# First layer, tile 0: half of the value rows gathered among the late key rows, inside tile 1's recurrence

## The chip, the core and the metric

The kernel is one program on one core of a Trainium2 chip. Its five engines work side by side and are ordered by semaphores alone: PE (TensorE, matmuls), DVE (VectorE), ACT (ScalarE), POOL (GpSimd, which issues the gathers here) and SP (SyncE, which issues the plain loads). The metric is device time in microseconds, from the first to the last instruction of the program with what lies around it; the median of several executions counts.

## What is computed

Two layers over 256 prompt tokens and 32 sample tokens: layer 0 mixes by an RWKV-7 recurrence, layer 1 by chunked gated linear attention, and after each stands a PEER mixer, in which every token has 8 heads x 16 = 128 experts. What the change touches is layer 0's recurrence for tile 1 and layer 0's PEER for tile 0:

```python
def step(S, inp):                       # RWKV-7, by token
    rt, wt, kt, vt, at, bt = inp
    sa = jnp.einsum('bhvk,bhk->bhv', S, at)
    S = S * wt[:, :, None, :] + sa[..., None] * bt[:, :, None, :] + vt[..., None] * kt[:, :, None, :]
    yt = jnp.einsum('bhvk,bhk->bhv', S, rt)
...
ue = jnp.take(u, expert, axis=0)        # PEER: key rows of the chosen experts
act = jax.nn.gelu(jnp.einsum('thed,td->the', ue, xt), approximate=False)
ve = jnp.take(v, expert, axis=0)        # and their value rows
return jnp.einsum('the,thed->td', (gate * act).astype(xt.dtype), ve)
```

## The kernel before, in words

The 288 tokens are three tiles: 0 and 1 of 128 prompt tokens, 2 (SAMPLE) with the 32 sample tokens in four copies. For a prompt tile each of the 128 experts of a token is one column: one gather by POOL brings 128 rows of 1024 float32 (0.52 MB), one for each token, into a slot of SBUF. Four gathers are a round. A tile has 32 key rounds (side 0, from `peer_u`) and 32 value rounds (side 1, from `peer_v`).

**The ring.** Until late in the program there are two groups of four slots. `round_at` gives every round its place n in the order of all rounds, `place_of(n)` its group; successive rounds alternate between the two. POOL walks the order in `gather` (line 721 issues) and, before it refills a slot, waits until that slot was used. Its queue is in order, so a gather that waits holds all behind it. For tile 0 of layer 0 all 32 key rounds stand before all 32 value rounds.

**Who uses the rows.** A key row is used by DVE in `row_product` (line 1125: one multiply and sum over 1024 columns). A value round is used by PE in `value_round`: eight matmuls of 32 lanes x 512 columns (line 1920) into `total`, which is PSUM banks 6 and 7. It waits for its four rows, and frees their slots as it goes through them.

**How they are spread.** Rows and rounds are no loops of their own: they are slipped into other work by a credit. On DVE `open_rows` opens a count and a rate, and `serve` spends rate x work whenever DVE is about to wait for a PSUM product (`fill`) or for ScalarE (`scalar_done`). On PE `open_values` does the same, and `serve` spends it ahead of each product for DVE (`for_vector`), each product for ScalarE (`for_scalar`) and each wait for operands (`operands`). With `paired`, only `fill` and `for_vector` spend credit, so that both engines count the same products. `rest_rows` and `rest_values` do what is left. Everything is decided when the program is built: on each engine the order is fixed.

**The place.** Tile 0's first 64 key columns are used during tile 1's input mixing. Then `core(1)` runs, tile 1's recurrence: for either half of the heads an attention part (five products for DVE), with the state and value matmuls behind each, then six levels of a triangular inverse (four products each, the last two) and the four closing products. In it DVE uses key columns 64 to 127 (`RATES["core1"]`, 1.9 rows for one unit of work). At its end PE opens the 32 value rounds at 0.5. `out(0, (1,))` follows: output product, norm, queries, scores and, in two halves, the choice of tile 1's experts; between scores and fan-out PE runs up to 6 more value rounds in each half, with 5 clock-raising matmuls behind each. A fan-out (`fan_out`) turns the chosen indices around for the value gathers; DVE waits for both (`experts_fanned`). Then comes `core(SAMPLE)`, which does the rest of the rounds before the sample's attention part, and in which DVE adds the sum of tile 0's experts (`add_experts`).

**PSUM banks.** ScalarE's products take two pairs of banks, (4, 5) and (6, 7), while `banks.two` holds, else the first alone. Since `total` is the second pair, `two` must be off when value rounds run. PE and ACT each keep their own count of it. Before, it goes off at the end of `core(1)`; with one pair, a product of 1024 columns waits until ScalarE has copied out the one before.

Of the kernel before, what the change touches and what calls it, by code (L numbers as in the profile page):

```python
# [54 lines left out]

MINGLED = ()

# [120 lines left out]
def program(nc, a, outs):  # L178
    (y_p, y_s, S_p, sh_p, G_p, S_s, sh_s, G_s) = outs
    with ExitStack() as ctx:  # L180
# [562 lines left out]
        def _(act):  # L743
# [119 lines left out]
            def core(t):  # L863

                sample = t == SAMPLE
                copy_out(wlog, D, func=ACT.Sigmoid)
                copy_out(bT, D, func=ACT.Sigmoid)
# [62 lines left out]
                if t == 1:  # L930
                    weights_due(0, 0, 1)
                    banks.two = False
                    copy_out(state_out[0][0:RK, :], D, RK)
                    act.dma_start(S_p[0, 0].rearrange("h v k -> v h k"),
                                  state_out[0][0:RK, :].rearrange("v (h k) -> v h k", k=RK)).then_inc(state_stored[0], 16)
                    nst[0] += 16
                    act.wait_ge(state_stored[0], nst[0])
# [150 lines left out]
        def _(dve):  # L1088
            w = Counts()
            stream = Share()  # L1090
            RATES = {"mix": 14, "core1": 1.9, "core2": 4.0, "enter": 6, "gla": 2.6, "out": 7}
            at = [0, 0, 0]
# [253 lines left out]
            def core(t):  # L1346
# [52 lines left out]
                if t == 1:  # L1399
                    weights_due(0, 0, 0)  # L1400
                    open_rows(0, 0, 64, 64, RATES["core1"])
                if sample:
# [411 lines left out]
        def _(pe):  # L1814
            w = Counts()
            banks, bufs, stream = Banks(), Buffers(), Share()
            at = [0, 0, 0]
            VALUE_RATES = {"out": 0.5, "gla": 0.5, "core2": 0.8}
            nfv, nfa = [0], [0]
# [203 lines left out]
            def core(t):  # L2023
# [3 lines left out]
                if t == 0:  # L2027
                    pe.wait_ge(pack_loaded, 16 * 5)
                    lora2, g2 = lora2_first, g2_first
                else:  # L2030
                    pack = weight(5)
                    bufs.kept = pack
                    lora2, g2 = pack_views(pack)
                for i in range(2):
# [62 lines left out]
                for group in groups_of(t):  # L2097
# [9 lines left out]
                    if t == 1:  # L2107
                        for hh, b in halves:
                            mark = turn_half(hh)
                            if hh == 0:  # L2110
                                fan_weights(0, 0, 0)
                            pe.wait_ge(scalar_drained, mark)
                            attention(b)
# [135 lines left out]
                if sample:  # L2249
                    open_values(0, 1, VALUE_RATES["out"])  # L2250
                if t == 1:
                    fan_weights(0, 0, 1)
                    banks.two = False
                    open_values(0, 0, VALUE_RATES["out"])
                    operands()
# [263 lines left out]
```

## Time and profile before

| | us |
|---|---|
| median of 3 executions (2941.88 to 2962.33) | 2942.13 |
| the profiled execution | 2945.39 |
| its span, first to last instruction | 2943.5 |
| PE busy | 1921.0 (65%) |
| DVE busy | 1594.7 (54%) |
| POOL busy | 1323.4 (45%) |
| ACT busy | 280.3 (10%) |
| chain that ended last: PE, DVE, DMA, POOL | 30%, 24%, 21%, 12% |

The granted TensorE clock was 0.809 of full speed in the mean. The profile names engines, lines and tiles; a wait is shown with the engine or transfer that ended it. Since no engine and no share of the chain dominates, the average says little: a change in one stage has to be read in that stage. In the rows, a value round is a row of PE with `128*32 128x512 x16` (each matmul of float32 counts twice there), a clock-raising matmul reads `pick,ident`.

### The profile page before, as it was taken

The page shows a single profiled execution, that of the slowest core. Times are in us where ns is not written, and L with a number is a line of the kernel's source. Part 1 is how long each engine was busy: PE and PEld are TensorE (multiplying, and loading weights), DVE is VectorE, ACT ScalarE, POOL GpSimd, SP SyncE. Part 2 cuts the span into 40 slices and gives each one's busy share as a digit, 9 for nine tenths or more (in the row PEclk, how much of TensorE's full clock was granted, in tenths as well). Part 3 has the DMA queues.
Part 4 walks back from the last instruction along what each step waited for, and adds up shares of the span by engine and source line. Part 5 has one row for each costly group of instructions (what it writes and reads, how often), then busy time and mean ns, then how long its engine had stood idle before and what let it go on. Part 6 is the DMA issues. An engine that isn't in the chain of part 4 may idle for free.

```text
span 2943.5 us, 26768 instructions
## 1 busy us (share of the span) xinstructions
PE 1921.0 (65%) x10173; PEld 1231.3 (42%) x10173; DVE 1594.7 (54%) x2987; ACT 280.3 (10%) x442; POOL 1323.4 (45%) x1160
## 2 busy tenths in 40 slices
PE   5879857837968776657577758678257764453533
PEld 2469523327945435445245227363135433350100
DVE  4253376566752826967412146865961738766033
ACT  1111000020110010010100110001100000000000
POOL 0000012543543555655334235556754675467774
PEclk8989979968789987767798888889568986776876
DMA  8430586964679897767999878789878998899998
GB/s 275 172 130 2 189 308 202 362 238 137 202 266 348 302 325 254 242 217 235 331 355 347 315 253 322 273 281 399 294 275 340 406 386 310 279 353 371 409 409 325
DMA packets 303482, 841.78 MB, mean 286 GB/s; under 512 B 46062, under 2 KB 57246, under 8 KB 303356
## 3 DMA queue, kind: packets, MB, share of 16 engines
q0 software_dynamic: 165888, 604.05, 56.1%
q1 hardware_dynamic: 126900, 231.65, 22.3%
q10 hardware_dynamic: 10568, 4.38, 0.6%
q8 instruction: 82, 1.34, 0.2%
q14 instruction: 44, 0.36, 0.0%
HBM read 829.68 MB, written 10.31 MB: 285 GB/s over the span
## 4 chain that ended last, share of the span: by engine, by line
PE 30%; DVE 24%; DMA 21%; POOL 12%; issue 7%; ACT 3%; PEld 1%; SPq 0%; ACTq 0%; DVEq 0%; PEldq 0%; POOLq 0%
PE psum L1920 28%; POOL arena L721 9%; DVE arena L1125 9%; DVE arena L1105 6%; DMA arena<-in_peer_v,idx_v 6%; POOL wring L721 3%; DMA wring<-in_ada_w 3%; DMA wring<-in_gla_w_in 3%; DMA wring<-in_rw_w_rkv 2%; DMA hc<-in_peer_v,idx_v 2%; DMA wring<-in_peer_wq 1%; PE psum L1938 1%; DVE hT L1105 1%; DMA out<-arena 1%; DMA wring<-in_peer_v,idx_u 1%
## 5 line engine op out<-in xcount | busy, mean ns | idle before, releaser
L721 POOL DMA_INDIRECT arena<-in_peer_u,idx_u x560 | 740.9, 1323 | 1062.1 <-DVE acts L1125 492.7
L1920 PE MATMUL psum<-arena 128*32 128x512 f32 (+6 forms) x3662 | 610.2, 557 | 447.8 <-DMA arena<-in_peer_v,idx_v 170.5
L1125 DVE CUSTOM_DVE_ANT_0 arena<-arena,hc 128x1024 f32<-128x1024 f32 x544 | 644.1, 1224 | 90.6 <-DMA arena<-in_peer_u,idx_u 64.5
L721 POOL DMA_INDIRECT arena<-in_peer_v,idx_v x428 | 422.1, 986 | 461.4 <-PE psum L1920 340.7
L1920 PEld LDWEIGHTS psum<-arena 128*32 128x32 f32 (+2 forms) x3662 | 323.5, 170 | 665.4 <-issue 477.8
L1920 PE MATMUL psum<-pick,ident 128*128 128x256 f32 x1090 | 272.7, 405 | 47.2 <-DVEq L1376 39.2
L1920 PEld LDWEIGHTS psum<-pick,ident 128*128 128x128 f32 x1090 | 215.3, 203 | 132.6 <-issue 54.0
L1920 PE MATMUL psum<-wring,arena 128*32 128x512 f32 (+3 forms) x728 | 213.9, 663 | 77.8 <-DMA wring<-in_peer_v,idx_v 43.0
L1920 PE MATMUL psum<-hT,wring 128*128 128x128 f32 (+3 forms) x1824 | 237.9, 293 | 17.0 <-ACT arena L767 6.3
L1920 PEld LDWEIGHTS psum<-hT,wring 128*128 128x128 f32 (+1 forms) x1824 | 225.7, 198 | 40.0 <-issue 21.9
L1920 PE MATMUL psum<-wring,hT 128*128 128x512 f32 (+1 forms) x480 | 192.2, 560 | 13.5 <-DMA wring<-in_gla_w_in 10.2
L767 ACT ACTIVATE arena<-psum 128x512 f32<-128x512 f32 (+6 forms) x125 | 97.3, 779 | 876.4 <-PE psum L1920 646.4
L1920 PEld LDWEIGHTS psum<-wring,arena 128*128 128x128 f32 (+2 forms) x728 | 85.6, 172 | 202.4 <-issue 182.6
L1920 PEld LDWEIGHTS psum<-wring,hT 128*128 128x128 f32 x480 | 90.0, 207 | 114.8 <-issue 100.0
L1105 DVE TENSOR_TENSOR arena<-arena 128x1024 f32<-128x1024 f32 (+4 forms) x148 | 124.8, 843 | 16.0 <-ACTq L1007 5.5
L1920 PE MATMUL psum<-wring,cT 128*32 128x512 f32 x384 | 65.0, 816 | 71.4 <-DMA wring<-in_ada_w 51.3
L1125 DVE CUSTOM_DVE_ANT_0 arena<-arena,psum 128x1024 f32<-128x1024 f32 x16 | 19.5, 1221 | 138.4 <-DMA arena<-in_peer_u,idx_u 137.7
L1245 DVE MAX8 arena<-psum 128x8 f32<-128x128 f32 x64 | 19.1, 299 | 137.3 <-PE psum L1920 135.0
L1105 DVE TENSOR_TENSOR arena<-psum,vring 128x1024 f32<-128x1024 f32 x12 | 14.7, 1223 | 136.1 <-PE psum L1920 93.1
L1938 PE MATMUL psum<-ident,arena 128*128 128x128 f32 x148 | 28.6, 359 | 80.6 <-DVEq L1633 42.6
L721 POOL DMA_INDIRECT wring<-in_peer_v,idx_v x64 | 61.3, 958 | 19.5 <-issue 19.5
L1105 DVE TENSOR_TENSOR arena<-arena,psum 128x512 f32<-128x512 f32 (+2 forms) x45 | 35.1, 780 | 58.4 <-PE psum L1920 57.1
(231 smaller groups left out, 1789.1 us busy)
## 6 DMA issues: line engine op xcount, KB each, us to landing
wring<-in_ada_w SPq DMA_DIRECT2D x24, 2048.0 KB
wring<-in_peer_wq SPq DMA_DIRECT2D x24, 2048.0 KB
wring<-in_rw_w_rkv SPq DMA_DIRECT2D x12, 2048.0 KB
wring<-in_gla_w_in SPq DMA_DIRECT2D x12, 2048.0 KB
wring<-in_rw_wo SPq DMA_DIRECT2D x6, 2048.0 KB
wring<-in_gla_wo SPq DMA_DIRECT2D x6, 2048.0 KB
vring<-mod_d SPq DMA_DIRECT2D x22, 512.0 KB
arena<-in_peer_u,idx_u POOLq DMA_INDIRECT x560, 6.2
```

The source lines that it names most:

```text
L721: pool.indirect_dma_start(slot(s, n), None, v_rows if side else u_rows, bass.IndirectOffsetOnAxis(index, 0)).then_inc(rows_landed[s], 16)
L767: done(act.activation(dst, shaped(fill(cols)[0:rows, :], dst), func, scale=scale), scalar_drained)
L1105: done(dve.tensor_tensor(out, i0, i1, op), s)
L1125: dve.tensor_tensor_reduce(slot(s, n), slot(s, n), hidden(li, t), 1.0, 0.0, MUL, ADD, acts[:, (3 * li + t) % 2, col:col + 1]).then_inc(row ...
L1245: done(dve.max(vals[:, 0:8], src))
L1920: return nc.tensor.matmul(out, lhsT, rhs, start=start, stop=stop)
L1938: last = nc.tensor.transpose(ps[:, k * P:(k + 1) * P], src[:, k * P:(k + 1) * P], ident[:])
```

## The change

It sets `MINGLED = ((0, 0),)`. In the order of rounds, tile 0's key rounds 16 to 31 and value rounds 0 to 15 then alternate. `core(1)` opens those 16 value rounds on PE right behind the first fan-out of key weights, paired, at 0.45 rounds for one product for DVE; DVE's key rows become paired as well, at 1.8. Rounds left over are done at the end of `core(1)`, and the other 16 value rounds are opened where all 32 were. ScalarE's products use one pair of banks from the start of `core(1)` on, on both engines.

```diff
-MINGLED = ()
+MINGLED = ((0, 0),)
...
             def core(t):
                 sample = t == SAMPLE
+                if t:
+                    banks.two = False
                 copy_out(wlog, D, func=ACT.Sigmoid)
...
                     weights_due(0, 0, 1)
-                    banks.two = False
...
-            RATES = {"mix": 14, "core1": 1.9, "core2": 4.0, "enter": 6, "gla": 2.6, "out": 7}
+            RATES = {"mix": 14, "core1": 1.8, "core2": 4.0, "enter": 6, "gla": 2.6, "out": 7}
...
-                    open_rows(0, 0, 64, 64, RATES["core1"])
+                    open_rows(0, 0, 64, 64, RATES["core1"], True)
...
-            VALUE_RATES = {"out": 0.5, "gla": 0.5, "core2": 0.8}
+            VALUE_RATES = {"core1": 0.45, "out": 0.5, "gla": 0.5, "core2": 0.8}
...
                     bufs.kept = pack
+                    banks.two = False
...
                                 fan_weights(0, 0, 0)
+                                open_values(0, 0, VALUE_RATES["core1"], 16, 0, True)
...
                 if t == 1:
+                    rest_values()
                     fan_weights(0, 0, 1)
-                    banks.two = False
-                    open_values(0, 0, VALUE_RATES["out"])
+                    open_values(0, 0, VALUE_RATES["out"], 16, 16)
```

POOL's gathers, in which the buffers of the ring are all named arena. Before, from the first one on:

```order
L721 DMA arena<-in_peer_u,idx_u 128x1024 x128
L721 DMA arena<-in_peer_v,idx_v 128x1024 x128
```

Now (where lines are left out, four gathers of either kind go on alternating):

```order
L721 DMA arena<-in_peer_u,idx_u 128x1024 x68
L721 DMA arena<-in_peer_v,idx_v 128x1024 x4
L721 DMA arena<-in_peer_u,idx_u 128x1024 x4
...
L721 DMA arena<-in_peer_v,idx_v 128x1024 x68
```

So 64 value gathers stand between key gathers, and a key gather now waits behind value gathers too.

PE in the third level of the recurrence: two level products for ScalarE (128x128), then four products for DVE (128x64). Before:

```order
L1920 MATMUL psum<-arena 128x128 x8
L1920 MATMUL psum<-wring,hT 128x128 x8
L1920 MATMUL psum<-arena,hT 128x64 x8
L1920 MATMUL psum<-hT,arena 128x64 x8
L1920 MATMUL psum<-arena,wring 128x64 x8
L1920 MATMUL psum<-wring,arena 128x64 x8
```

Now, with two value rounds (32x512) ahead of two of the products:

```order
L1921 MATMUL psum<-arena 128x128 x8
L1921 MATMUL psum<-wring,hT 128x128 x8
L1921 MATMUL psum<-arena,hT 128x64 x8
L1921 MATMUL psum<-arena 32x512 x8
L1921 MATMUL psum<-hT,arena 128x64 x8
L1921 MATMUL psum<-arena,wring 128x64 x8
L1921 MATMUL psum<-arena 32x512 x8
L1921 MATMUL psum<-wring,arena 128x64 x8
```

There are 16 such rounds between the first attention part's second product and the last product of the recurrence: two in each attention part, twelve behind.

PE from the last scores of `out(0, (1,))` to the sample's mixing (a value round is 32x512, `arena,pick` is a fan-out, `wring,arena` the sample's first product). Before, from the last round of the first half's choice on:

```order
L1920 MATMUL psum<-arena 32x512 x8
L1920 MATMUL psum<-pick,ident 128x256 x5
L1920 MATMUL psum<-arena,pick 128x64 x4
L1920 MATMUL psum<-arena 32x512 x8
L1920 MATMUL psum<-pick,ident 128x256 x5
...
L1920 MATMUL psum<-arena 32x512 x8
L1920 MATMUL psum<-arena,pick 128x64 x4
L1920 MATMUL psum<-wring,arena 128x512 x2
L1920 MATMUL psum<-arena 32x512 x8
L1920 MATMUL psum<-wring,arena 128x512 x2
```

Now, from the third and last round of that half on:

```order
L1921 MATMUL psum<-arena 32x512 x8
L1921 MATMUL psum<-pick,ident 128x256 x5
L1921 MATMUL psum<-arena,pick 128x64 x8
L1921 MATMUL psum<-wring,arena 128x512 x4
L1921 MATMUL psum<-arena,le 128x512 x2
```

The second half's fan-out follows the first's, and the sample's mixing starts, with no value round between.

## Rows read from the trace of the kernel before

**Rows 1.** Stages: us, busy of each engine, granted clock, DMA share, GB/s.

```profile
core 0: us, PE busy (x) PEld busy (x) DVE busy (x) ACT busy (x) POOL busy (x), PEclk, DMA share, GB/s
661.50:746.00 84.50, 66.44 (x365) 63.25 (x366) 48.28 (x61) 6.88 (x13) 25.41 (x20) 0.76 0.38 125
746.00:842.00 96.00, 86.62 (x662) 85.66 (x661) 81.07 (x126) 13.74 (x15) 58.51 (x44) 0.87 0.72 241
...
1022.00:1060.00 38.00, 25.21 (x133) 11.67 (x132) 0.85 (x4) 1.68 (x6) 19.69 (x21) 0.87 0.84 300
```

**Rows 2.** Chain of work that ended last: start, us, what.

```profile
1033.79 6.13 DMA arena<-in_peer_v,idx_v
...
1047.45 6.47 DMA arena<-in_peer_v,idx_v
```

**Rows 3.** Order of time, PE, the expert choice: start, us, matmuls, idle before, releaser.

```profile
1000.33 1.92 PE L1920 MATMUL psum<-arena 128*32 128x512 f32 x16 [2.08 <-DMA arena<-in_peer_v,idx_v]
...
1012.33 1.93 PE L1920 MATMUL psum<-arena 128*32 128x512 f32 x16 [1.02 <-DMA arena<-in_peer_v,idx_v]
...
1026.40 3.42 PE L1920 MATMUL psum<-arena 128*32 128x512 f32 x16 [3.73 <-DMA arena<-in_peer_v,idx_v]
...
1054.06 3.24 PE L1920 MATMUL psum<-arena 128*32 128x512 f32 x16 [4.02 <-DMA arena<-in_peer_v,idx_v]
1057.23 1.10 PE L1920 MATMUL psum<-arena,pick 128*128 128x64 f32 x8
```

**Rows 4.** Order of time, POOL, value gathers in the same stage.

```profile
1014.48 1.88 POOL L721 DMA_INDIRECT arena<-in_peer_v,idx_v  x1 [1.47 <-PE psum L1920]
...
1030.07 0.94 POOL L721 DMA_INDIRECT arena<-in_peer_v,idx_v  x1 [4.51 <-PE psum L1920]
1031.31 0.94 POOL L721 DMA_INDIRECT arena<-in_peer_v,idx_v  x1 [0.30 <-issue]
```

**Rows 5.** Order of time, DVE, from the second half's indices to the sample's mixing.

```profile
1021.33 0.19 DVE L1700 CAST idx_u<-arena 128x64 uint32<-128x64 f32 x1
...
1059.71 0.23 DVE L1751 CAST idx_v<-arena 128x128 uint32<-128x128 f32 x1 [36.60 <-ACTq L983]
1073.35 1.23 DVE L1105 TENSOR_TENSOR arena<-arena,vring 128x1024 f32<-128x1024 f32 x1 [13.41 <-DMA vring<-in_rw_kk]
...
1081.86 0.17 DVE L1108 TENSOR_SCALAR s<-s 128x16 f32<-128x16 f32 x1 [4.67 <-ACTq L772]
...
1103.35 1.23 DVE L1105 TENSOR_TENSOR arena<-psum,vring 128x1024 f32<-128x1024 f32 x1 [3.31 <-PEq L1852]
```

**Rows 6.** DMA issues, 746 to 842, then 975 to 1060: count, median us to landing.

```profile
arena<-in_peer_u,idx_u POOLq DMA_INDIRECT x36, 5.8
...
arena<-in_peer_v,idx_v POOLq DMA_INDIRECT x51, 6.2
```

**Rows 7.** Order of time, PE, first level's products and the closing ones.

```profile
748.38 1.90 PE L1920 MATMUL psum<-arena,hT 128*128 128x64 f32 x16
750.12 1.95 PE L1920 MATMUL psum<-hT,arena 128*128 128x64 f32 x16
...
832.17 9.10 PE L1920 MATMUL psum<-arena 128*128 128x64 f32 x80
```

**Rows 8.** Order of time, ACT, the copy of a level's first product.

```profile
761.98 1.02 ACT L767 ACTIVATE arena<-psum 128x1024 f32<-128x1024 f32 x1 [12.31 <-PE psum L1920]
```

**Rows 9.** Order of time, attention parts: POOL's gathers, DVE's and PE's last products.

```profile
673.95 1.68 POOL L721 DMA_INDIRECT arena<-in_peer_u,idx_u  x1 [0.64 <-DVE acts L1125]
...
676.02 2.05 PE L1920 MATMUL psum<-arena 128*128 128x128 f32 x16 [1.50 <-DVE hc L1105]
...
681.85 1.22 DVE L1105 TENSOR_TENSOR hc<-psum,le 128x1024 f32<-128x1024 f32 x1
...
713.10 1.68 POOL L721 DMA_INDIRECT arena<-in_peer_u,idx_u  x1 [20.39 <-DVE acts L1125]
...
723.40 1.22 DVE L1105 TENSOR_TENSOR hc<-psum,le 128x1024 f32<-128x1024 f32 x1
```

## The prediction

> **What bounds the kernel now.** I read the stage table first, then the chain of work that ended last, then the order of time on PE, POOL and DVE. Around the change no one engine is the bound everywhere [rows 1]. In the levels of tile 1's recurrence (746 to 842) PE is busy 86.62 of 96 us and DVE 81.07; the DMA engines have a share of 0.72, and only key rows fly. In the two attention parts (661.5 to 746) the DMA share is 0.38. Later it turns over: from 1022 to 1060 DVE is busy 0.85 of 38 us. There the chain alternates between value gathers in flight and PE's rounds: a last gather of four flies 6.13 us, the next one's 6.47 [rows 2], and a round follows when its four rows have landed, 12.0 us after the round before it in the same four slots (1000.33 to 1012.33) or 14.07 (1012.33 to 1026.40) [rows 3]. PE fans out the second half's expert indices only at 1057.23, behind six such rounds [rows 3], though DVE had written that half by 1021.33 + 0.19 = 1021.52; DVE then waits 36.60 us [rows 5]. So the value rows are short of time there, and the recurrence has DMA time over. The change trades one against the other.
>
> **What it gives.** Of 32 value rounds 16 move into the recurrence. Behind it stand the same 13 rounds up to the last score product, then 3 instead of 6 in the first half's choice, 0 instead of 6 in the second's, and 0 instead of 7 around the fan-out and in the start of the sample's mixing. Terms:
> - The second fan-out follows DVE's write at 1021.52 and not the round of 1054.06: about 1022 instead of 1057.23, 35 us.
> - DVE's start into the sample's mixing then waits 13.41 us for rw_kk [rows 5], behind a semaphore that comes with the fan-out; it moves along. Its next wait, 4.67 us for ScalarE's root, hangs on PE products among which two rounds stood: between 0 and 4.67, I take 4, since both rounds leave.
> - The 3.31 us in which DVE waited for the last value sum [rows 5] go: the last of the 32 rounds then stands third in the first half's choice, long before.
> Together 42 us. Bounds: 35 + 0 + 3.3 = 39 and, with the whole 4.67 and a rw_kk load that is somewhat quicker without gathers beside it, 46. The DMA work is not less: the moved gathers just fly earlier.
>
> **What it costs.** The 36 PSUM products between PE and DVE in the recurrence (10 of attention, 20 of levels one to five, 2 of level six, 4 at the end) pace both sides: 1.8 key rows and 0.45 value rounds each. Key and value rounds alternate in the gather order, so from here on key rows live in one group of four slots and value rows in the other. There is no second group for values: a round's four gathers can start only when PE has used the round before, and POOL, in order, issues them only behind the four key gathers ahead of them.
>
> The price of that loop, from rows: POOL starts 0.27 us after a round's end (1030.07 after 1026.40 + 3.42); gathers start 1.24 us apart at best (0.94 + 0.30), three steps are 3.72 [rows 4]; the last lands 5.8 us after its issue in the levels, 6.2 later on (medians) [rows 6]; the round is 1.92 us at full clock, 3.42 otherwise [rows 3]. Sum 11.7 at best. Measured loops of this kind are 12.0 and 14.07 [rows 3], the long one when a gather took 1.88 us instead of 0.94 [rows 4]. In the levels POOL is such a POOL: 58.51 us for 44 gathers is 1.33 each [rows 1], and eight of 1.33 + 0.30 are 13.0 us per key and value round. I take 13.0, between the two measured loops and with POOL's own price.
>
> Levels: value round 4 stands ahead of the second product of level one, now at 750.12; round 15 stands ahead of the last product, which now starts at 832.17 + 24/40 of 9.10 = 837.6 [rows 7] (24 of its row's 40 matmuls come before it). Between lie 11 loops: 750.12 + 11 x 13.0 + 1.92 = 895.0, against 837.6: **+57 us**. DVE's rows (1.8 instead of 1.9 per product) and PE's own work fit inside: 2.2 products between rounds are some 8 of the 13 us on DVE (81.07 us over 26 products is 3.1 each, and a level's rows get fewer).
>
> Attention: round 0 is there early, round 1 is wanted before the fifth product. POOL may start on it only after the key gather of 673.95, which waited for the fourth key row: 675.93, three steps of 1.24 to 1.98, 5.8 in flight, a round of 1.92 to 3.42, a product of 2.05: 689 to 693, where DVE took that product at 681.85: +7.5 to +11. In the second half the same from the gather of 713.10, with two products behind: 731 to 734 against DVE's 723.40: +7 to +11 [rows 9]. Twice 9: **+18 us**. PE's stretches between (state and values) do not shorten.
>
> The single PSUM pair: the second level product of a pair now waits for ScalarE's copy of the first (starts at 761.98, 1.02 long [rows 8]); with the hand-overs I put it at 1.4 us, six times, 8 in all, and twice for the turns. I cost it at nothing, since PE waits for value rows in each loop anyway; without that cover it would be 8.
>
> Sum: 18 + 57 - 42 = **+33 us**. The profiled execution took 2945.39 us (span 2943.5), 3.3 above the median of 2942.13. I add the difference to the median: 2975 us.
>
> **A rule against the trace.** Thirteen loops (11 in the levels, one in each attention part) each hold a gather's flight of 5.8 us [rows 6]. The Trainium skill, DMA: Bandwidth & Descriptors, section "Anatomy of one DMA — SWDGE (gpsimd) path", fits a DMA from GpSimd as 2.0 us plus its bytes at 436 GB/s; for 0.52 MB that is an estimate of 3.2 us, 2.6 less than the row. By it the loop would be 10.4 and the change would come out even. The row decides, since it counts from POOL's issue to the landing, as the loop does.
>
> **Rivals.** With a loop of T us the cost is 18 - 2 x (13 - T) + 750.12 + 11 T + 1.92 - 837.6 = 13 T - 93.6, and the change costs nothing at T = 10.4.
> - *Loop at its floor* (T = 12.0): cost 62, net +20, 2962. For it: rounds at full clock and gathers of 0.94 do run so [rows 3, 4]. Against: in the levels a gather takes 1.33 on average [rows 1].
> - *Even*: shorter flights or partial overlap bring T to 10.4 or so: net 0, 2942. For it: DMA share only 0.72 [rows 1]. Against: flights are 5.8 us under that light load [rows 6]. (The fit of the Trainium skill above would give this case.)
> - *Faster*: the moved rounds fall into DMA time that is idle, and the recurrence hardly stretches. It decides at T = 8.2, where the cost is 13 and the net -29: 2913 us; at the 7.8 us that the 11 loops have today (837.6 - 750.12 = 87.5, less a round, over 11) it would be the whole gain less the attention parts. For it: 0.38 and 0.72 of DMA share. Against: a loop holds a flight, three steps and a round, 11.7 at best.
> - *POOL slowed throughout* (T = 14.07): cost 89, net +47, 2989. For it: the row of 1.88 and the 1.68 of the attention part [rows 4, 9]. This is the upper end of the forecast's case.
>
> **How the numbers follow.** A change of 1% is 29 us, about what a measurement of this kernel tells from none; slower by over 1% begins at T = 12.7. Of the measured loops' spread (12.0 to 14.07) two thirds lie above. Chances: loop of 12.7 to 14.1, my forecast, 0.52; floor case 0.26; even case 0.14; faster 0.08. So faster 0.08, within 1% 0.40, slower 0.52. The range reaches from the even case (2944) to the slow loop with the smaller gain (2942 + 89 - 39 = 2992); what is left out is the faster case, a little of the even one and something above. The forecast's own part of it is 2971 to 2992.
>
> **What the changed profile would show.** Right: the stretch from the first attention product to the second half's key weights (661.5 to 843) about 75 us longer; in it PE waiting for in_peer_v rows ahead of nearly each value round, same-slot rounds 12 to 14 us apart, DVE waiting for PE's PSUM; DMA share near 0.8 there; the 36.60 us wait on the second fan-out gone to about 1 or 2; no value round behind the first half's choice; from the recurrence's end to the first attention product of the sample's mixing about 42 us less. Wrong: rounds less than 12 us apart, so the loop is not what binds; PE waiting for vector_drained or for ScalarE's copies rather than for rows; or a gain that ends before DVE's start into the sample's mixing because a load (rw_kk, recurrent rows) arrives no earlier.

## The result, and the profile after

| | before | after |
|---|---|---|
| median, us | 2943.47 (4 executions, 2941.88 to 2962.33) | 3023.15 (4 executions, 3014.87 to 3028.63) |
| span of the profiled execution, us | 2943.5 | 3018.7 |
| granted TensorE clock, mean | 0.809 | 0.794 |

The ratio is 1.0238, with a 95% interval of 1.0204 to 1.0271: the change costs 2.4%, some 70 us. The two medians lie 79.7 us apart, which is the upper end of that interval; the two profiled spans differ by 75.2. The kernel before is itself not steady to better than 29 us: over all its executions, those of the experiments included, it took 2940 to 2970 us, so each ratio compares a kernel with runs of before on the same chip.

Stages after (columns as in [rows 1]): the attention parts, the levels with the closing products, the stretch up to the second fan-out, the start of the sample's mixing.

```profile
core 0: us, PE busy (x) PEld busy (x) DVE busy (x) ACT busy (x) POOL busy (x), PEclk, DMA share, GB/s
662.80:768.40 105.60, 72.24 (x418) 59.58 (x417) 47.79 (x59) 6.88 (x13) 36.82 (x35) 0.73 0.50 174
768.40:944.40 176.00, 116.18 (x864) 87.66 (x864) 84.90 (x130) 13.73 (x15) 102.45 (x93) 0.83 0.79 273
944.40:1124.60 180.20, 109.47 (x690) 64.85 (x690) 88.36 (x247) 12.93 (x22) 62.80 (x64) 0.82 0.75 272
1124.60:1182.00 57.40, 24.82 (x71) 15.96 (x72) 29.03 (x35) 14.17 (x20) 5.54 (x4) 0.50 0.28 90
```

Where the forecast had all of the recurrence's added time in waits for rows, PE waits for two things there: the rows of value rounds, and ScalarE's copies. What PE waited for from the first attention product to the second half's key weights, in sum, times and longest, before:

```profile
PE psum L1920 <- DVEq L1434: 8.8, 2, 5.0
PE psum L1920 <- DVE hT L1105: 8.4, 5, 2.3
...
PE psum L1920 <- ACT hT L767: 2.1, 1, 2.1
```

And after:

```profile
PE psum L1921 <- DMA arena<-in_peer_v,idx_v: 70.8, 11, 11.7
PE psum L1921 <- ACT arena L767: 9.5, 8, 1.3
...
PE psum L1939 <- ACT arena L853: 2.6, 1, 2.6
```

70.8 us for value rows are new, and so are ScalarE's copies: 9.5 + 2.6 and two smaller ones (1.2 and 0.8) are 14.1 us, where before only one of 2.1 us stood.

Order of time on PE after, levels three to six (columns as in [rows 3]; value rounds are the rows of 128x512):

```profile
836.94 1.92 PE L1921 MATMUL psum<-arena 128*32 128x512 f32 x16 [0.18 <-DMA arena<-in_peer_v,idx_v]
...
853.72 3.26 PE L1921 MATMUL psum<-arena 128*32 128x512 f32 x16 [6.02 <-DMA arena<-in_peer_v,idx_v]
...
867.31 3.29 PE L1921 MATMUL psum<-arena 128*32 128x512 f32 x16 [6.62 <-DMA arena<-in_peer_v,idx_v]
...
880.65 1.92 PE L1921 MATMUL psum<-arena 128*32 128x512 f32 x16 [1.21 <-ACT arena L767]
...
893.15 3.64 PE L1921 MATMUL psum<-arena 128*32 128x512 f32 x16 [6.86 <-DMA arena<-in_peer_v,idx_v]
896.72 2.32 PE L1921 MATMUL psum<-arena,wring 128*128 128x64 f32 x16
898.88 1.95 PE L1921 MATMUL psum<-wring,arena 128*128 128x64 f32 x16
900.66 2.00 PE L1921 MATMUL psum<-arena 128*128 128x128 f32 x16
903.93 2.02 PE L1921 MATMUL psum<-wring,hT 128*128 128x128 f32 x16 [1.26 <-ACT arena L767]
905.79 1.90 PE L1921 MATMUL psum<-hT,arena 128*128 128x64 f32 x16
907.62 1.92 PE L1921 MATMUL psum<-arena 128*32 128x512 f32 x16
```

A loop here is the time from the start of one value round to the start of the next. Value round 4 starts at 779.23 and round 15 at 935.04: 155.8 us over 11 loops, 14.16 each, where 13.0 was forecast. (In the two kernels below with the same recurrence, choice_fillers and choice_fillers_70, they were 15.0 and 15.2.) Three kinds of loop are seen. From 853.72 to 867.31 (13.6 us) the rows are awaited for 6.62 us, as forecast. From 893.15 to 907.62 (14.5 us) nothing is awaited but ScalarE's copy: PE's own chain over a level's border fills the loop. And from 836.94 to 853.72 (16.8 us) the gathers started late, as they did in the first loop (779.23 to 795.58, 16.4 us); these two are 7.1 us of the 12.8 by which the eleven loops exceed 11 x 13.0. POOL in that loop:

```profile
838.64 1.68 POOL L721 DMA_INDIRECT arena<-in_peer_u,idx_u  x1 [4.01 <-DVE acts L1126]
...
842.49 1.56 POOL L721 DMA_INDIRECT arena<-in_peer_v,idx_v  x1 [0.30 <-issue]
```

Round 8 had freed its slots by 838.9, but the next value gather stood behind two key gathers, the first of which had waited 4.01 us for DVE to use a key row. DVE in turn waits for key rows that were gathered late:

```profile
855.33 1.23 DVE L1126 CUSTOM_DVE_ANT_0 arena<-arena,hc 128x1024 f32<-128x1024 f32 x1 [7.51 <-DMA arena<-in_peer_u,idx_u]
```

So each side holds up the other through the one queue. The chain of work that ended last goes through that place, from DVE's use of a key row over POOL and the flight to PE, and further on through a copy by ScalarE (start, us, what):

```profile
837.13 1.23 DVE arena L1126
...
838.64 1.68 POOL arena L721
...
847.01 6.57 DMA arena<-in_peer_v,idx_v
...
853.72 3.25 PE psum L1921 x13
...
860.95 6.23 DMA arena<-in_peer_v,idx_v
...
867.31 8.86 PE psum L1921 x64
...
876.26 1.03 ACT arena L767
```

Behind the recurrence, PE at the second fan-out and DVE from there to the last value sum (answers to [rows 3, 5]):

```profile
1124.65 1.97 PE L1921 MATMUL psum<-arena,pick 128*128 128x64 f32 x8 [31.60 <-DVEq L1704]
...
1132.85 3.78 PE L1921 MATMUL psum<-wring,arena 65*128 65x512 f32 x4 [1.11 <-ACT arena L767]
```

```profile
1128.00 0.23 DVE L1752 CAST idx_v<-arena 128x128 uint32<-128x128 f32 x1 [1.96 <-ACTq L984]
1137.09 1.23 DVE L1106 TENSOR_TENSOR arena<-arena,vring 128x1024 f32<-128x1024 f32 x1 [8.86 <-DMA vring<-in_rw_kk]
...
1151.85 0.17 DVE L1109 TENSOR_SCALAR s<-s 128x16 f32<-128x16 f32 x1 [10.91 <-ACTq L772]
...
1170.34 1.23 DVE L1106 TENSOR_TENSOR arena<-psum,vring 128x1024 f32<-128x1024 f32 x1 [0.32 <-DVE arena L1386]
```

The fan-out now waits for DVE, the 36.60 us wait is 1.96, and the last value sum is there in time (the 0.32 us are a wait of DVE for itself). But DVE's wait for ScalarE's root grew from 4.67 to 10.91 us.

### The profile page after: what moved, and what is told of

It reads as the page before. It is cut to its first block, busy times and chain, and to the rows that moved or that the text cites. A ratio compares the mean times of both kernels' runs of the same rounds, so it can differ in the third digit from the quotient of the medians.

```text
span 3018.7 us, 26509 instructions
## 1 busy us (share of the span) xinstructions
PE 1898.3 (63%) x10043; PEld 1204.3 (40%) x10043; DVE 1596.4 (53%) x2987; ACT 280.2 (9%) x442; POOL 1314.0 (44%) x1160
## 3 DMA queue, kind: packets, MB, share of 16 engines
q8 instruction: 81, 1.33, 0.2%
## 4 chain that ended last, share of the span: by engine, by line
PE 30%; DVE 25%; DMA 22%; POOL 11%; issue 6%; ACT 4%; SPq 1%; PEld 1%; ACTq 0%; DVEq 0%; PEldq 0%; POOLq 0%
PE psum L1921 28%; POOL arena L721 9%; DVE arena L1126 8%; DVE arena L1106 7%; DMA arena<-in_peer_v,idx_v 6%; DMA wring<-in_gla_w_in 3%; DMA wring<-in_ada_w 2%; POOL wring L721 2%; DMA wring<-in_rw_w_rkv 2%; DMA wring<-in_peer_wq 2%; DMA vring<-mod_d 1%; PE psum L1939 1%; ACT arena L767 1%; DMA out<-arena 1%; DVE hT L1106 1%
## 5 line engine op out<-in xcount | busy, mean ns | idle before, releaser
L721 POOL DMA_INDIRECT arena<-in_peer_u,idx_u x560 | 725.1, 1295 | 1150.9 <-DVE acts L1126 575.8
L1921 PE MATMUL psum<-arena 128*32 128x512 f32 (+6 forms) x3662 | 607.7, 557 | 490.4 <-DMA arena<-in_peer_v,idx_v 212.6
L1921 PE MATMUL psum<-pick,ident 128*128 128x256 f32 x960 | 238.0, 403 | 36.8 <-DVEq L1377 28.9
L1921 PEld LDWEIGHTS psum<-pick,ident 128*128 128x128 f32 x960 | 188.8, 202 | 104.9 <-issue 40.2
L1921 PE MATMUL psum<-wring,hT 128*128 128x512 f32 (+1 forms) x480 | 191.7, 559 | 22.1 <-DMA wring<-in_gla_w_in 11.2
L1106 DVE TENSOR_TENSOR arena<-arena,psum 128x512 f32<-128x512 f32 (+2 forms) x45 | 35.1, 780 | 76.5 <-PE psum L1921 75.2
L1939 PEld LDWEIGHTS psum<-ident,arena 128*128 128x128 f32 x148 | 24.8, 197 | 118.0 <-DVEq L1634 43.8
```

The source lines that it names most:

```text
L721: pool.indirect_dma_start(slot(s, n), None, v_rows if side else u_rows, bass.IndirectOffsetOnAxis(index, 0)).then_inc(rows_landed[s], 16)
L1106: done(dve.tensor_tensor(out, i0, i1, op), s)
L1921: return nc.tensor.matmul(out, lhsT, rhs, start=start, stop=stop)
L1939: last = nc.tensor.transpose(ps[:, k * P:(k + 1) * P], src[:, k * P:(k + 1) * P], ident[:])
```

## The experiments

All stages are read between the same instructions in each profile: **recurrence**, from PE's first attention product to the second half's key weights; **choice**, from there to DVE's cast of the second half's indices; **start**, from the cast to where DVE takes the first attention product of the sample's mixing; the **rest**, to the end of the span. Each is a difference of start times. The ratio is to the kernel before on the same chip, with its 95% interval.

| kernel | recurrence | choice | start | rest | ratio |
|---|---|---|---|---|---|
| before | 182.0 | 216.2 | 55.5 | 1828.3 | |
| after | 281.7 | 183.6 | 53.8 | 1836.9 | 1.0238 (1.0204 to 1.0271) |
| pair_only | 196.6 | 212.6 | 58.8 | 1836.5 | 1.0060 (1.0037 to 1.0082) |
| gain_only | 183.8 | 184.3 | 53.5 | 1838.4 | 0.9870 (0.9835 to 0.9906) |
| rounds_no_gathers | 202.5 | 183.6 | 53.8 | 1827.7 | 0.9971 (0.9947 to 0.9994) |
| values_first | 325.4 | 184.2 | 53.5 | 1837.2 | 1.0350 (1.0308 to 1.0392) |
| rows_waited_one_pair | 271.6 | 185.1 | 53.6 | 1845.5 | 1.0178 (1.0128 to 1.0228) |
| rows_waited_two_pairs | 261.3 | 187.6 | 53.7 | 1838.2 | 1.0145 (1.0097 to 1.0193) |
| no_keys_one_group | 256.7 | 184.0 | 53.8 | 1844.1 | 1.0145 (1.0094 to 1.0195) |
| no_keys_two_groups | 176.9 | 184.0 | 53.4 | 1843.8 | 0.9883 (0.9825 to 0.9942) |
| eight_rounds | 232.2 | 182.5 | 52.5 | 1834.4 | 1.0088 (1.0062 to 1.0113) |
| early_fan_only | 182.5 | 186.5 | 86.2 | 1848.1 | 1.0001 (0.9983 to 1.0020) |
| fillers_ahead | 283.3 | 184.7 | 53.4 | 1834.1 | 1.0250 (1.0203 to 1.0296) |
| choice_fillers | 294.3 | 186.2 | 53.4 | 1839.2 | 1.0248 (1.0214 to 1.0281) |
| choice_fillers_70 | 288.7 | 184.9 | 52.6 | 1828.3 | 1.0236 (1.0195 to 1.0276) |
| keys_then_values | 187.0 | 187.8 | 52.0 | 1833.8 | 0.9922 (0.9897 to 0.9947) |

Readings of the table itself. The rest varies between 1828 and 1848 us in kernels that do the same there; the 8.6 us between before and after lie within that. And the changed recurrence, the same in three of these kernels up to its end (after, choice_fillers, choice_fillers_70), took 281.7 to 294.3 us, so a single profile settles no difference under some 13 us in it. Where no value round stands in the recurrence it is steadier: before, gain_only and early_fan_only, which do the same there, took 182.0 to 183.8 us.

**The sum taken apart: pair_only, gain_only, rounds_no_gathers.** The first two are edits of the kernel before.

```diff
# pair_only, in ACT's core(t); in PE's the second line, behind bufs.kept = pack
+                if t:
+                    banks.two = False
...
# gain_only: the ring's places move up by 16, POOL starts at value round 16
+LEFT_OUT = 16
...
+    return n - LEFT_OUT if (li, t, side) > (0, 0, 0) else n
...
-                    open_values(0, 0, VALUE_RATES["out"])
+                    open_values(0, 0, VALUE_RATES["out"], LEFT_OUT, LEFT_OUT)
...
# rounds_no_gathers, from the changed kernel: as gain_only, and in value_round
+                fixed = not phase and r < LEFT_OUT
-                for j in range(GRP):
+                for j in range(0 if fixed else GRP):
                     pe.wait_ge(rows_landed[g * GRP + j], 16 * (use + 1))
...
```

> The kernel before with one pair of PSUM banks for ScalarE from the start of core(1) on, and nothing else of the change. The forecast cost this at nothing behind the value rows, and at 8 us without that cover, so by it this kernel takes about 2951 us (2943 + 8), the time lying between the turns and the sixth level; the answering stages keep their lengths. Rival, the single pair is a main cause of the 80 us: each ScalarE product of the recurrence then waits 1.3 to 2.6 us for its copy (as rows of the changed kernel show ahead of some products), which over some 20 products in a chain would give 25 us or more, 2968 us or above.

> The kernel before with value rounds 0 to 15 of tile 0 left out altogether, gathers and matmuls (half of the value sum is missing): the gain of the move without its cost. By the forecast's sum 42 us less, 2901 us. By the trace of the changed kernel, in which the first attention product of the sample's mixing has gained 34 us behind the recurrence, 2909 us; if the further 8 us that it loses by its end come with the move too, 2917 us. A PE clock that falls while PE has no rounds in the expert choice would show as products of 3.7 us instead of 2 at the start of the sample's mixing, here too.

> The changed kernel in which the 16 mingled value rounds multiply a constant tile, without gathers and without waiting for rows (half of the value sum is wrong): single pair, paired rates and PE's matmuls stay, the loop of gather and round goes. If that loop is the cause (theory), the recurrence is back near its length before: 8 us for the pair and, since PE is busy 87 of 96 us in the levels, 10 to 20 us for 12 rounds of 1.9 to 3.4 us; with 34 to 42 us of gain 2915 to 2940 us. If PE's added work or the single pair is the cause (rival), most of the 100 us in the recurrence stays: 2980 us or more.

pair_only took 2971.07 us against 2955.25, 0.6% more: the recurrence is 14.6 us longer, between the 8 of the forecast and the 25 of the rival. Its waits for copies in the recurrence are 12.8 us: these, and again two of 1.2 and 0.8:

```profile
PE psum L1921 <- ACT arena L767: 8.2, 7, 1.3
...
PE psum L1939 <- ACT arena L853: 2.6, 1, 2.6
```

gain_only took 2920.15, 1.3% less; its stages lose 32 us in the choice and 2 in the start, 34 together and not 42. rounds_no_gathers took 2946.09, 0.3% less: recurrence +20.5, gain as in gain_only. So of the 99.7 us that the recurrence grew, single pair, paired rates and PE's matmuls by themselves are worth 20.5, and the other 79 come with the gathers. The theory held in kind; the pair was no zero.

**Which loop: values_first, the rows_waited pair, the no_keys pair.** All are edits of the changed kernel.

```diff
# values_first: POOL (round_at likewise)
-                        gather(li, t, 0, r)
...
                             gather(li, t, 1, r - rounds // 2)
+                        gather(li, t, 0, r)
# rows_waited_one_pair: value_round, rounds 0 to 15
+                if wait_only:
+                    for j in range(GRP):
+                        pe.sem_inc(rows_used[g * GRP + j], 1)
-                for h in range(2):
+                for h in range(0 if wait_only else 2):
# rows_waited_two_pairs: besides, banks.two goes off where it did before the change
# no_keys_two_groups (LEFT_OUT = 16, no MINGLED): key rounds 16 to 31 neither gathered nor used
-                        gather(li, t, 0, r)
+                        if li or t or r < LEFT_OUT:
+                            gather(li, t, 0, r)
...
-                    open_rows(0, 0, 64, 64, RATES["core1"], True)
+                    open_rows(0, 0, 64, 0, RATES["core1"], True)
# no_keys_one_group: besides, in places()
-        g = among[turn % len(among)]
+        g = 1 if LEFT_OUT <= n < 2 * LEFT_OUT else among[turn % len(among)]
```

> The changed kernel with each mingled value round gathered ahead of its key round instead of behind it. A round's four gathers then no longer stand behind four key gathers whose slots DVE has yet to free. If value gathers held up behind key gathers make the loop 14.2 us instead of the 13.0 forecast (theory: both sides coupled by the one queue), the loop falls to 12.7 to 13 and the time to 3005 to 3012 us. If the loop is flight, steps and round alone (rival), it stays at 14.2 and the time within 5 us of 3023. If key rows, now a round later, become the late ones, it gets longer: 3030 us or more.

> The changed kernel in which the 16 mingled value rounds wait for their rows and free the slots, but multiply nothing (half of the value sum is missing). The loop loses its round, 1.9 to 3.4 us of 14.2, thirteen times: some 32 us less than the changed kernel, 1.3% over the kernel before. It is also the base for the next run, which differs in the PSUM pair alone.

> As the run before it (value rounds that only wait and free), but ScalarE keeps both pairs of PSUM banks until the end of core(1), as before the change. The forecast held that PE's waits for rows cover the single pair: then this takes the same time, within 4 us. Rival, the cover doesn't hold and the pair's price comes on top of the loop: 15 to 20 us less, as the pair cost when it was changed alone.

> The changed kernel without key rounds 16 to 31 (neither gathers nor products, half of the key sums are zero); the 16 mingled value rounds keep one group of four slots. What is left of the loop is its floor: 0.27 + 3 x 1.24 + 5.8 + 1.92 = 11.7 us instead of 14.2. If value gathers held up behind key gathers make up the rest (theory), the levels get 11 x 2.5 = 27 us shorter and the time is 2985 to 2995 us, 1.3 to 1.7% over before. If one group is the whole cause (rival), the loop stays at 14 and the time near 3023 us. The gathers left out also make the stages behind a little quicker in neither case.

> As the run before it (no key rounds 16 to 31), but the mingled value rounds alternate between both groups of four slots. If the missing second group is what makes PE wait (theory), a round's rows are then under way while the round before is used: PE's waits for value rows go nearly away, and the time falls below the kernel before: gain 35, single pair and rounds some 20, so about 2925 us, 60 or more below the run before it. If the DMA engines or POOL's issue bound the rounds (rival), it stays within 20 us of that run.

values_first, 3.5% over before, is the worst of all, as the last of its three cases had it: to let values go first makes the key rows the late ones. PE's waits for value rows fell from 70.8 to 40.1 us, and PE waits for DVE instead (33.1 us in the two largest groups), since DVE's waits for key rows rose from 28.6 us to 130.3:

```profile
DVE arena L1126 <- DMA arena<-in_peer_u,idx_u: 130.3, 17, 12.8
```

Without the matmuls I expected 32 us less than after; the recurrence lost 10 (271.6), which is inside what the same recurrence varies by. From the first level's second product for DVE on it took 163.6 us, after the change 163.4. PE still waits for rows (74.3 us), now because of the keys. In rows_waited_two_pairs, POOL and PE near the end of the recurrence:

```profile
892.48 1.68 POOL L721 DMA_INDIRECT arena<-in_peer_u,idx_u  x1 [4.28 <-DVE acts L1125]
894.47 1.57 POOL L721 DMA_INDIRECT arena<-in_peer_v,idx_v  x1 [0.30 <-issue]
```

```profile
905.32 10.48 PE L1924 MATMUL psum<-arena 128*128 128x64 f32 x48 [7.52 <-DMA arena<-in_peer_v,idx_v]
```

A value gather waits for a key slot, the key slot for DVE, DVE for a product, and the product stands behind the value round that waits for this gather: a second loop, through both engines, about as long as the first. With both pairs of banks the recurrence was 10.3 us shorter again. That would be the pair's price beside waits for rows, but it is inside the same variation and the two ratios' intervals overlap, so neither the 4 us of the forecast nor the 15 to 20 of the rival is decided. What is firm is that the copies' waits are in the changed kernel undiminished (14.1 us, 12.8 in pair_only).

Without keys the second loop is gone, and in one group the loop should have fallen to 11.7 us. The time, 1.45% over before, came out as the theory of held-up value gathers had it (1.3 to 1.7%), but not for its reason: of the 25 us that the recurrence lost against after, 20.6 lie ahead of the first level's second product for DVE, most of that in the attention parts, and the levels' loop was still 13.7 us (round 4 at 757.09, round 15 at 908.17). PE there:

```profile
797.23 3.64 PE L1925 MATMUL psum<-arena 128*32 128x512 f32 x16 [2.84 <-DMA arena<-in_peer_v,idx_v]
800.80 3.68 PE L1925 MATMUL psum<-wring,arena 128*128 128x64 f32 x16
804.27 3.03 PE L1925 MATMUL psum<-arena 128*128 128x128 f32 x16
808.57 2.02 PE L1925 MATMUL psum<-wring,hT 128*128 128x128 f32 x16 [1.26 <-ACT arena L770]
810.43 1.90 PE L1925 MATMUL psum<-arena,hT 128*128 128x64 f32 x16
812.16 1.95 PE L1925 MATMUL psum<-hT,arena 128*128 128x64 f32 x16
814.04 1.92 PE L1925 MATMUL psum<-arena 128*32 128x512 f32 x16
```

This loop of 16.8 us waits for no rows: five products and a copy fill it, and the round and the first two products took 3.64, 3.68 and 3.03 us where the later ones took 1.9 to 2.0. Others in the same profile are 12.0 (757.09 to 769.09). What stands between two rounds is uneven, and a loop lasts as long as the longer of its two sides, so the mean lies above either side's own. With both groups the waits for rows are gone altogether (the view of PE's waits has no line for them) and the recurrence is 176.9 us, 80 below the same kernel with one group. (That it is below the 182.0 of before is no gain of the order: DVE's work on 64 key columns is left out too.) The two kernels differ in the group alone, so without keys the missing second group, which the forecast named, is shown as the cause of the waits; in the levels the rival (one group alone, keys or not) is nearer than the theory that keys make up the rest.

**Fewer rounds, and the fan-out alone.**

```diff
# eight_rounds (EARLY = 8; PE opens 8 at 0.225): POOL, behind key round r
+                            if r % 2:
+                                gather(li, t, 1, (r - rounds // 2) // 2)
# both: ahead of the second fan-out
-                        for _ in range(min(stream.left, 6 if tiles[0] else 6 - 2 * half)):
+                        for _ in range(min(stream.left, (6, 2)[half] if tiles[0] and li == 0 else 6 if tiles[0] else 6 - 2 * half)):
```

> The changed kernel with 8 value rounds instead of 16 in the recurrence, one behind every two key rounds (so that successive value rounds take either group), at 0.225 for a product; of the 24 behind it two instead of six stand ahead of the second fan-out. If the price is the loop of gather and round (theory), there are now 4.5 products or some 15 us between two value rounds, no less than the 14.2 of the loop: PE hardly waits for rows, and the recurrence is longer by the single pair and the rounds alone, some 18 to 20 us instead of 100. With the second fan-out 35 us earlier the time is 2925 to 2932 us, 0.4 to 0.6% below before. Rival: twelve gathers in one queue, 1.33 + 0.30 us each, make 19.6 us for each loop, then the recurrence is 40 us or more longer and the time 2950 us or more.

> The kernel before with two instead of six value rounds ahead of the second fan-out, and no round moved into the recurrence; eleven rounds instead of seven are left for the sample's mixing. The rows come no sooner, and the sample's attention waits for all rounds: the second fan-out is 35 us earlier, but the sample's attention starts within 4 us of where it did, so the time is that of the kernel before, within 0.3%. If the early fan-out alone brought the gain (rival), it would be 25 to 35 us less, 1% below.

eight_rounds was no gain but 0.9% over before: 50 us on the recurrence, not 20. PE still waited 28.3 us for rows, five times, although a loop was now longer than 14 us (20.6 to 27.3 in the levels): value gathers waited for key slots that DVE had not yet used. POOL, ahead of the round of 771.32:

```profile
766.24 1.67 POOL L722 DMA_INDIRECT arena<-in_peer_v,idx_v  x1 [22.36 <-DVE acts L1128]
```

My theory of a loop of fixed length had left out that second dependence. The rival's numbers (40 us or more, 2950 or more) were met, but POOL, whose issues by it leave no pause, waited some 80 us for DVE in this recurrence, so its price per gather alone is not the reason. early_fan_only came out as expected, with the time of before. Its second fan-out is early and DVE waits for the last value sum instead:

```profile
1106.71 1.23 DVE L1105 TENSOR_TENSOR arena<-psum,vring 128x1024 f32<-128x1024 f32 x1 [34.53 <-PEq L1852]
```

**The clock.**

```diff
# fillers_ahead, value_round
+                if phase == 0 and r in (5, 7, 9, 10, 12, 14, 15):
+                    raise_clock(8)
# choice_fillers, ahead of the second fan-out (choice_fillers_70: 70)
+                        if half and li == 0 and tiles[0] == 1:
+                            raise_clock(40)
```

> The changed kernel with eight clock-raising matmuls ahead of the wait for rows of value rounds 5, 7, 9, 10, 12, 14 and 15, those before which PE waited 4.5 us or more. If the clock that falls while PE waits makes the loop longer than its floor (rounds of 3.3 us instead of 1.92), seven loops lose 1.4 us each and some more in the products behind: 10 to 15 us less than the changed kernel, 1.9% over before. If the landing of the rows alone sets the loop's length (rival), no difference over 4 us.

> The changed kernel with 40 clock-raising matmuls ahead of the second fan-out, where PE idles 31.6 us. If the lost part of the gain (a wait of 10.9 us for ScalarE's root at the start of the sample's mixing, 4.7 before the change) comes from PE at half clock behind that idle time, products of 3.75 us turn to 1.9 and DVE's start into the sample's mixing gets 5 to 7 us shorter; the time falls by as much. If the wait stays at 10 us, the cause is another.

> The changed kernel with 70 instead of 40 clock-raising matmuls ahead of the second fan-out, at 0.43 us each 30 of the 31.6 us in which PE idles there. If PE at half clock behind the idle time is what lost part of the gain, the first four products behind the fan-out take 1.9 to 2.2 us instead of 3.75, and from the fan-out to ScalarE's root it is 20 to 22 us instead of 27.2. If that stretch stays at 27, the cause is another.

fillers_ahead brought nothing that shows (1.0250 against 1.0238; the intervals would hide 10 us), though PE's waits for rows fell from 70.8 to 48.0 us and four of the seven rounds ran in 1.92 us: the loops were 14.4 us all the same, so filled time was still waited time. The 40 fillers left 14.57 us of idle time and tested nothing. The 70 did fill the gap, and the fan-out ran at full clock, but the stage behind it soon fell back (PE, in order of time):

```profile
1105.35 30.44 PE L1921 MATMUL psum<-pick,ident 128*128 128x256 f32 x140
1135.62 1.00 PE L1921 MATMUL psum<-arena,pick 128*128 128x64 f32 x8
1137.99 2.70 PE L1921 MATMUL psum<-wring,arena 65*128 65x512 f32 x4 [1.37 <-ACT arena L801]
1141.80 3.78 PE L1921 MATMUL psum<-wring,arena 65*128 65x512 f32 x4 [1.11 <-ACT arena L767]
```

From fan-out to ScalarE's root it took 25.2 us, after the change 27.2, before 24.6, against 20 to 22 expected. So idle time ahead explains part of it at most; in early_fan_only, where value rounds still stand between these products, the same stretch took 23.4 (1030.64 to 1054.01). The sixteen profiles divide by the rounds: in the five kernels with value rounds among these products the stretch took 23.4 to 25.0 us at a granted clock of 0.76 to 0.91, in the eleven without them 25.2 to 27.2 us at 0.50 to 0.57. That the rounds kept PE's clock up fits this, but fillers between the products were not tried.

**Keys first, then values.** From the kernel before:

```diff
# DVE, behind each attention part of core(1)
+                            if t:
+                                rows_now(10)
...
# PE (and ACT without the last line), at the start of level 4; "core1" is 0.45
+                            if t and k == 4:
+                                banks.two = False
+                                open_values(0, 0, VALUE_RATES["core1"], 6, 0, True)
...
# the other 26 at the end of core(1), two of them ahead of the second fan-out
+                    rest_values()
+                    open_values(0, 0, VALUE_RATES["out"], 26, 6)
```

> The kernel before in which DVE uses ten more key rows behind each attention part of tile 1's recurrence, where it idles some 20 us, so that the keys are done earlier; six value rounds follow from the fourth level on, behind all keys and in both groups of slots, with one PSUM pair from there on; of the 26 behind it two instead of six stand ahead of the second fan-out. If alternating with keys is what made the rounds wait (theory), PE waits little for rows here, the recurrence is 10 to 18 us longer (three of six waits for the single pair, six rounds of 2 to 3.5 us), the second fan-out comes 33 us earlier and the time is 2920 to 2930 us where before is 2943, 0.4 to 0.8% below. If the recurrence has no time for value rounds in any order (rival), it is 33 us longer or more, and the time that of the kernel before or above it.

2931.02 us against 2953.87, 0.8% less than before, 0.5 to 1.0% by the interval, and faster than both kernels. The recurrence is 5 us longer, against 10 to 18 expected, the choice 28 us shorter, and the start another 3.5. PE's waits there for copies and rows:

```profile
PE psum L1928 <- ACT arena L767: 3.8, 3, 1.3
...
PE psum L1928 <- DMA arena<-in_peer_v,idx_v: 0.4, 1, 0.4
```

So the recurrence does have time for value rounds, six of them here, if they don't alternate with keys; the eight rounds of eight_rounds, which do, cost 50 us there. (This run changes DVE's key rows, the number of rounds and their order at once, so how much of it each is worth is not shown; the early fan-out alone brings nothing, by early_fan_only.) The granted clock was 0.95 in its levels, 0.87 before [rows 1].

## Why the prediction was wrong

The direction and what binds were right, the size was not: forecast +33 (2975, range to 2992), measured +70 by the ratio and +80 by the medians. By the profiles it is +65 up to the sample's first attention product: 99.7 from the recurrence, less 34.4 from choice and start, against 75 and 42. So 25 us were missed on the cost and 8 on the gain. The remainder, 10 us by the two profiled spans, lies in parts that vary by 20 us between kernels that are the same there; what it comes from stays open.

The step that failed is the cost of the recurrence, 18 + 57 + 0 = 75 where 99.7 was measured: the single PSUM pair was put at nothing, and the loop at 13.0 us from POOL's price, with PE's own chain and the wait of key gathers for DVE taken to fit inside it.

- **What bounds, and the gain's first term: right.** 33.6 us between second key weights and second fan-out (213.8 before, 180.2 after) against 35, and the wait of 3.31 us for the last value sum is gone.
- **Gain, ScalarE's root: wrong in sign.** Forecast 4 us less; from fan-out to root it became 27.2 instead of 24.6. PE's products there run at the lower of the two clock levels, 1.2 GHz (granted clock 0.50), in every kernel without value rounds among them and without fillers ahead. Gain 34 instead of 42, in gain_only as well.
- **The single pair at nothing: failed.** "PE waits for value rows in each loop anyway" does not cover it. Two level products with the copy between them stand in five of the eleven loops, those over a level's border. In two of these PE still waits for rows behind them (6.02 us at 853.72); in the other three it waits for them 0.18 us (836.94) or not at all (880.65, 907.62), so the copy is in PE's own chain. In the attention parts the copies stand at turns and first level, where PE waits for no rows (the rounds of 723.71 and 779.23 follow without a wait). By itself the pair is worth 14.6 us, 6.1 up to the first level's second product for DVE and 8.5 behind it, by the profile of pair_only; its waits are all in the changed kernel. What it is worth beside the waits for rows is not settled.
- **The loop at 13.0: mis-sized, 14.16 measured, and for a reason of its own.** The flight (5.8) and the floor held: value rows landed in 5.6 us in the median, and loops of 12.0 (no_keys_one_group) and 12.5 (after) occur. By the rule of the Trainium skill that the prediction weighed (DMA: Bandwidth & Descriptors, "Anatomy of one DMA — SWDGE (gpsimd) path") an estimate of 3.2 us stood against the 5.8 us of the row; the trace after, with its 5.6 us, does not agree with that estimate either. POOL's price, on which 13.0 rested, was lower than taken: 102.45 us for 93 gathers are 1.10 each, not 1.33, so eight with their gaps are 11.2. That 13.0 came as near as it did is luck. What made loops long was what the prediction had put inside: PE's chain between rounds, which is uneven ("PE's own work fit inside", but it fills 14.5 us at 893.15), and value gathers held behind key gathers that wait for DVE (16.4 and 16.8).
- **Attention 18: 27.9 measured.** The first part's last product was taken by DVE at 693.86 instead of 681.85, 10.8 us later when the later start is taken off, within the forecast 7.5 to 11. Of the 9.9 too few 6.1 are the pair's, by pair_only.
- **Levels 57: 72.0 measured.** 11 x 1.16 = 12.8 us more for the loops and 1.6 for the last round, which took 3.56 us and not 1.92, account for it. What the pair costs in the levels lies inside these loops and is not added to them.
- **The rivals.** The slow loop's number (14.07) was met, but not its reason, POOL slowed throughout. The rows_waited and no_keys runs suggest why no single remedy helped: two loops of like length, one through the single group, one through both engines and the queue, and to remove one leaves the other.

Of the signs that were to show the forecast wrong, one showed in part: PE waits for ScalarE's copies besides the rows. How the 79 us of the gathers divide between the two loops in the changed kernel stays open; the runs take away one at a time, and either then sets the pace.

## What to carry to other kernels

When two streams share an in-order queue and a ring, alternating them gives each half of the slots and lets either one's late consumer stop the other; put them one behind the other where the order of use allows it, which paid here for six rounds. A loop between engines is as long as the longer of its sides each time round, so work it out at the worst place between two rounds, not from the mean. Call a wait "covered" only after finding, for every place where it stands, the other wait that is longer there.

## What was not expected of the hardware

- In the levels after the change a value round took 1.92 us when PE had waited up to 2.7 us ahead of it, and 3.26 to 3.64 after waits of 4.5 us or more. The wait alone does not decide: before, one took 3.42 after 3.73 [rows 3], and in no_keys_one_group one took 3.64 after 2.37.
- 30.4 us of back-to-back matmuls did not hold the clock for the sparse stage behind them: the second product behind the fan-out was back at 3.78 us, and the stretch up to the root had a granted clock of 0.57.
- One gather takes POOL 0.94 us in most cases, but 1.47 to 1.99 in about a fifth of the cases in the levels after.
